# MLP output product by seven block products of eight, with sums of weight blocks made in DRAM by accumulating transfers

## What is computed

```python
h = rms_norm(x, pre_norm_mlp[l])
y = jnp.square(jax.nn.relu(h @ w_mlp_in[l])) @ w_mlp_out[l]   # (512, 4096) @ (4096, 1024)
x = x + rms_norm(y, post_norm_mlp[l])
```

## Time and profile before

| | |
|---|---|
| device time, median of three runs | 775.53 us (775.46 to 775.83) |
| span of the profiled execution, first to last instruction | 773.7 us |
| so outside the span, against the median | 1.8 us |
| PE busy | 765.9 us, 99% of the span |
| DVE, ACT, POOL busy | 329.9, 353.1, 387.1 us |
| data moved | 77.27 MB, mean 100 GB/s |

### The profile page before, as it was taken

The page is one execution under the profiler, slowest core; times in us unless marked ns, Lnnn a source line. Parts: engine busy times, 40 slices in busy tenths (PEclk is TensorE's granted clock), DMA queues, the critical chain, the costliest instruction groups (busy, mean ns, idle before and its releaser), DMA issues.

```text
span 773.7 us, 12234 instructions
## 1 busy us (share of the span) xinstructions
PE 765.9 (99%) x4276; PEld 628.5 (81%) x4276; DVE 329.9 (43%) x497; ACT 353.1 (46%) x625; POOL 387.1 (50%) x342
## 2 busy tenths in 40 slices
PE   9999999999999999999999999999999999999996
PEld 7788778888877878888888888888888888888885
DVE  5896899952544555546407210111013222222125
ACT  6656842286654464546336623333234333333333
POOL 2348884424437533664455545444544444444444
PEclk9999999999999999999999999999999999999999
DMA  9335233313222212223721333323332322222222
GB/s 332 97 97 190 63 88 96 98 53 97 56 55 63 74 43 56 83 96 117 265 81 55 95 109 96 93 83 108 95 96 95 105 98 95 95 95 95 95 81 110
DMA packets 59401, 77.27 MB, mean 100 GB/s; under 512 B 4544, under 2 KB 43616, under 8 KB 59360
## 3 DMA queue, kind: packets, MB, share of 16 engines
q1 hardware_dynamic: 59024, 76.44, 31.1%
q10 hardware_dynamic: 336, 0.28, 0.1%
HBM read 74.59 MB, written 2.11 MB: 99 GB/s over the span
## 4 chain that ended last, share of the span: by engine, by line
PE 91%; POOL 3%; DVE 2%; ACT 2%; issue 0%; DMA 0%; SPq 0%; ACTq 0%; POOLq 0%; DVEq 0%
PE bank L530 28%; PE bank L532 27%; PE bank L531 27%; POOL rsq L1598 2%; PE bank L755 1%; PE bank L778 1%; POOL w_lo L1604 1%; PE bank L765 1%; DVE y_out L1252 1%; PE bank L719 1%; DVE tmp L1516 1%; PE bank L683 1%; PE bank L560 1%; PE bank L730 1%; PE bank L827 0%
## 5 line engine op out<-in xcount | busy, mean ns | idle before, releaser
L1604 POOL TENSOR_TENSOR w_lo<-raw,w_hi 128x512 fp32r<-128x512 f32 x241 | 310.6, 1295 | 360.8 <-ACT w_hi L951 359.1
L951 ACT ACTIVATE w_hi<-raw 128x512 fp32r<-128x512 f32 (+1 forms) x246 | 153.3, 629 | 259.5 <-PE bank L532 254.4
L530 PE MATMUL bank<-h_hi,w_hi 128*128 128x512 f32 (+1 forms) x528 | 208.3, 395 | 0.1
L531 PE MATMUL bank<-h_lo,w_hi 128*128 128x512 f32 (+1 forms) x528 | 204.1, 387 | 0.0
L532 PE MATMUL bank<-h_hi,w_lo 128*128 128x512 f32 (+1 forms) x528 | 204.0, 386 | 0.0
L530 PEld LDWEIGHTS bank<-h_hi,w_hi 128*128 128x128 f32 x528 | 99.2, 188 | 24.8 <-issue 4.0
L532 PEld LDWEIGHTS bank<-h_hi,w_lo 128*128 128x128 f32 x528 | 99.2, 188 | 20.6
L531 PEld LDWEIGHTS bank<-h_lo,w_hi 128*128 128x128 f32 x528 | 99.3, 188 | 18.8
L530 PE MATMUL bank<-w_hi,a_hi 128*128 128x512 f32 x256 | 99.7, 389 | 0.1
L532 PE MATMUL bank<-w_hi,a_lo 128*128 128x512 f32 x256 | 99.6, 389 | 0.0
L531 PE MATMUL bank<-w_lo,a_hi 128*128 128x512 f32 x256 | 99.6, 389 | 0.0
(11 more groups left out here) (250 smaller groups left out, 888.0 us busy)
## 6 DMA issues: line engine op xcount, KB each, us to landing
raw<-in_w_in SPq DMA_DIRECT2D x87, 256.0 KB, 2.8
raw<-in_w_mlp_out SPq DMA_DIRECT2D x64, 256.0 KB, 2.5
raw<-in_w_mlp_in SPq DMA_DIRECT2D x62, 256.0 KB, 2.7
raw<-in_w_out SPq DMA_DIRECT2D x16, 256.0 KB, 2.7
x_sb<-in_x SPq DMA_DIRECT2D x4, 512.0 KB, 7.7
decay<-row_copy SPq DMA_DIRECT2D x4, 512.0 KB, 6.0
raw<-in_w_branch_att SPq DMA_DIRECT2D x8, 256.0 KB, 2.6
raw<-in_w_branch_dn SPq DMA_DIRECT2D x8, 256.0 KB, 2.7
```

Of the source, the lines that this page charges most:

```text
L530: pe.matmul(o, s_hi, m_hi, start=start, stop=False, skip_group_check=True)
L531: pe.matmul(o, s_hi, m_lo, start=False, stop=False, skip_group_check=True)
L951: return a.activation(o, i_, ACT.Copy, scale=scale)
L1604: g.tensor_tensor(w_lo[:, slot, :], raw[:, slot, :], w_hi[:, slot, :].bitcast(F32), ALU.subtract).then_inc(lo_ready, 1)
```

## The change

The output product is written as a 2 x 2 block product. A, the activations, is cut into token halves and into even and odd k-blocks of 128; B, the weights, into even and odd k-blocks and column halves (`w2_block(i, kappa, half)`). Seven block products are made instead of eight. The seven need sums of weight blocks and differences of activation blocks:

- v1 = B00 + B01, t3 = B11 + B01, t2 = v1 + B11, t4 = t2 + B10, each 2048 x 512 floats (4 MB) in DRAM, in eight pieces of 512 KB. Per piece and sum SP issues a DRAM to DRAM copy and POOL an accumulating transfer onto it: 32 of each. `SUM_AT` puts them at units 12 + 11 i + (0, 1, 8, 16) of the mixer, i = 0 to 7: the copy on SP behind the load of that unit, the add on POOL behind the subtraction for that unit. The copies of t2 and t4 wait for the add of v1 and of t2; every add waits for its copy. SP waits for all adds of v1, t3 and t2 before the first load of the output product, and for t4's before its second stage.
- Activations: `act` holds six blocks of 256 tokens per pair of k-blocks. ACT's squares write four of them, DVE makes three of 128x256 in `combine` during MLP in, and a fourth later (`s4`).
- The product has two stages in place of one. Stage one (`one`, eight turns): per turn two pairs of k-blocks by four weight parts, 8 parts of 6 matmuls. Stage two (`two`, seven turns and a tail): per turn 6 parts of 6 matmuls; the tail has 36 matmuls, ordered by output block. A **part** is a 128x512 weight tile; there are 64 + 48 = 112 of them where there were 64 units. Matmuls: 112 x 6 = 672 in place of 64 x 12 = 768.
- In both stages w_lo moves from POOL to DVE, two parts in one 128x1024 instruction; ACT's w_hi likewise. The parts have eight slots (`raw`, `raw_b`, `raw_c`), a_hi and a_lo are 128x1024 in stage one and 128x768 in stage two.
- Between the stages ACT copies two banks out and DVE makes six sums; after stage two the output blocks are put together by eight DVE additions, and squares, gain and residual follow per block.

The core of the diff:

```diff
 U_M1 = U_OUT + 64
-U_ALL = U_M1 + 64
+NI = 8
+S_TWO = 64
+N_SUM = 8
+SUM_AT = {12 + 11 * i + (0, 1, 8, 16)[q]: (q, i) for i in range(N_SUM) for q in range(4)}
...
-    act = at("act", 112, [P, FF // P, S])
+    act = at("act", 112, [P, 14, 6, 256])
+    act_end = at("act_end", 68, [P, 2, 6, 256])
...
+    v1_sum, t3_sum, t2_sum, t4_sum = [nc.dram_tensor(f"{name}_sum", (FF // 2, 512), F32).ap() for name in ("v1", "t3", "t2", "t4")]
+    w2 = w_mlp_out[0]
+    def w2_block(i, kappa, half):
+        c, n = slice(half * 512, half * 512 + 512), FF // N_SUM
+        return w2[i * n:i * n + n, c].rearrange("(j k p) c -> k p j c", k=2, p=P)[kappa]
+    def t_block(t, i):
+        n = FF // 2 // N_SUM
+        return t[i * n:i * n + n, :].rearrange("(j p) c -> p j c", p=P)
+    def t_copy(q, i):
+        t = (v1_sum, t3_sum, t2_sum, t4_sum)[q]
+        source = (w2_block(i, 0, 0), w2_block(i, 1, 1), t_block(v1_sum, i), t_block(t2_sum, i))[q]
+        return t_block(t, i), source
+    def t_add(q, i):
+        t = (v1_sum, t3_sum, t2_sum, t4_sum)[q]
+        return t_block(t, i), (w2_block(i, 0, 1), w2_block(i, 0, 1), w2_block(i, 1, 1), w2_block(i, 1, 0))[q]
...
             load(u, u % RAW, unit_source(u), u - RAW + 1 if u >= RAW else None)
+            if u in SUM_AT:
+                q, i = SUM_AT[u]
+                if q > 1:
+                    sp_.wait_ge(t_added[2 * q - 4], 16 * (i + 1))
+                sp_.dma_start(*t_copy(q, i)).then_inc(t_copied[q], 16)
...
+        def one_source(i, s):
+            n = i * 2 + s // 4
+            return (w2_rows(n, 0, 0), t_rows_of(t2_sum, n), t_rows_of(t3_sum, n), t_rows_of(v1_sum, n))[s % 4]
+        def two_source(i, s):
+            n = i * 2 + s // 3
+            return (w2_rows(n, 1, 0), w2_rows(n, 1, 1), t_rows_of(t4_sum, n))[s % 3]
...
-        def mlp_out_part(j, t, start, stop):
-            c = slice(t * P, t * P + P)
-            return three(bank[2 * t + j % 2][:], a_hi[:, j // 2, c], a_lo[:, j // 2, c], w_hi[:, j % 4, :],
-                         w_lo[:, j % 4, :], start, stop)
-        def mlp_out(i, first, last):
-            for j in range(4 if last else 8):
-                if j % 2 == 0:
-                    pe.wait_ge(alo_ready, i * 4 + (j // 2 + 1))
-                pe.wait_ge(lo_ready, i * 8 + (U_M1 + j - 1))
-                for t in (2, 3, 0, 1):
-                    if first and j == 0 and t < 2:
-                        pe.wait_ge(relu_done, 30 + 2 * t)
-                    x_ = mlp_out_part(j, t, first and j < 2, False)
-                x_.then_inc(unit_done, 1)
...
+        def product(bank0, p, c, i2, s, start, stop):
+            w0 = c * 256 + i2 * P
+            return three(bank[bank0 + i2][:], a_hi[p][:, w0:w0 + P], a_lo[p][:, w0:w0 + P], *w_part(s), start, stop)
+        def one(i, first=False, last=False):
+            for p in range(2):
+                pe.wait_ge(alo_ready, i * 2 + (p + 1))
+                for c in range(4):
+                    s = 4 * p + c
+                    pe.wait_ge(part_lo, i * 8 + (s + 1))
+                    if first and p == 0 and c > 1:
+                        pe.wait_ge(relu_done, 30 if c == 2 else 32)
+                    for i2 in range(2):
+                        x_ = product((4, 6, 0, 2)[c], p, c, i2, s, first and p == 0, last and p == 1)
+                    x_.then_inc(part_done, 1)
+        def two(i, first=False):
+            for p in range(2):
+                pe.wait_ge(alo_ready, i * 2 + (2 * NI + p + 1))
+                for c in range(3):
+                    s = 3 * p + c
+                    pe.wait_ge(part_lo, i * 6 + (S_TWO + s + 1))
+                    if first and p == 0:
+                        pe.wait_ge((p1_copied, x_made, y_made)[c], 2)
+                    for i2 in range(2):
+                        x_ = product((4, 6, 0)[c], p, (1, 0, 2)[c], i2, s, first and p == 0, False)
+                    x_.then_inc(part_done, 1)
+        one(0, True)
+        with pe.Fori(1, NI - 1) as i:
+            one(i)
+        one(NI - 1, False, True)
+        two(0, True)
+        with pe.Fori(1, NI - 1) as i:
+            two(i)
+        pe.wait_ge(alo_ready, 4 * NI)
+        for c, i2 in ((2, 0), (2, 1), (0, 0), (1, 0), (0, 1), (1, 1)):
+            for p in range(2):
+                s = {2: 0, 0: 2, 1: 6}[c] + p
+                if i2 == 0:
+                    pe.wait_ge(part_lo, S_TWO + 6 * (NI - 1) + {2: 2, 0: 4, 1: 0}[c] + p + 1)
+                x_ = product((4, 6, 0)[c], 2 * p, (1, 0, 2)[c], i2, s, False, p == 1)
+            x_.then_inc(tail_done, 1)
...
+        def two(i, before):
+            for g in range(3):
+                a.wait_ge(part_done, before + 2 * g + 2)
+                if g:
+                    a.wait_ge(s4_ready, i * 2 + g)
+                    a_split(i * 2 + (g - 1), g - 1, slice(3, 6))
+                w_split(2 * g, 2, i * 16 + (16 * (NI + 1)))
...
+        last_two = S_TWO + 6 * (NI - 2)
+        a.wait_ge(s4_ready, 2 * NI)
+        a_split(2 * NI - 1, 2, slice(3, 6))
+        w_split(6, 2, 16 * (NI + 1))
+        a.wait_ge(part_done, last_two + 2)
+        w_split(0, 2, 16 * (2 * NI))
+        a.wait_ge(part_done, last_two + 4)
+        a_split(2 * NI - 2, 0, slice(3, 6))
...
+        def combine(n):
+            x = [act_pair(n, slice(s, s + 1)).rearrange("p a c -> p (a c)") for s in range(6)]
+            v.tensor_tensor(x[3], x[2], x[5], ALU.subtract).then_inc(comb_one, 1)
+            v.tensor_tensor(x[2], x[0], x[2], ALU.subtract)
+            v.wait_ge(comb_one, n + 1)
+            v.tensor_tensor(x[1], x[0], x[3], ALU.subtract).then_inc(comb_ready, 1)
+        def s4(n):
+            x = [act_pair(n, slice(s, s + 1)).rearrange("p a c -> p (a c)") for s in (1, 4, 3)]
+            v.tensor_tensor(x[2], x[0], x[1], ALU.subtract).then_inc(s4_ready, 1)
+        def a_low(n, b, slots, ready):
+            c = slice(0, (slots.stop - slots.start) * 256)
+            v.wait_ge(ahi_ready, ready)
+            v.tensor_tensor(a_lo[b][:, c], act_row(n, slots), a_hi[b][:, c].bitcast(F32), ALU.subtract).then_inc(alo_ready, 1)
+        def w_low(s, n, ready):
+            v.wait_ge(part_hi, ready)
+            h, l = w_parts(s, n)
+            v.tensor_tensor(l, raw_part(s, n), h.bitcast(F32), ALU.subtract).then_inc(part_lo, n)
+        def one(i):
+            for g in range(4):
+                w_low(2 * g, 2, i * 8 + (2 * g + 2))
+                if g % 2:
+                    a_low(i * 2 + g // 2, g // 2, slice(0, 4), i * 2 + (g // 2 + 1))
+        def two(i):
+            for p in range(2):
+                s4(i * 2 + p)
+            for g in range(3):
+                if g:
+                    a_low(i * 2 + (g - 1), g - 1, slice(3, 6), i * 2 + (2 * NI + g))
+                w_low(2 * g, 2, i * 6 + (S_TWO + 2 * g + 2))
...
+        relu(NI - 1, ms=(0, 1))
+        combine(2 * NI - 4)
+        combine(2 * NI - 3)
+        a_low(0, 0, slice(0, 4), 1)
+        for s in range(3):
+            w_low(s, 1, s + 1)
+        relu(NI - 1, ms=(2, 3))
+        w_low(3, 1, 4)
+        w_low(4, 2, 6)
+        a_low(1, 1, slice(0, 4), 2)
+        w_low(6, 2, 8)
+        for n_ in (2 * NI - 2, 2 * NI - 1):
+            v.wait_ge(act_ready, 2 * n_ + 2)
+            combine(n_)
+        with v.Fori(1, NI - 1) as i:
+            one(i)
+        one(NI - 1)
...
+        def times_norm(t, half):
+            c = slice(half * 512, half * 512 + 512)
+            mark(v.tensor_tensor(y_out[:, t, c], half_of(t, half), pn_mlp[:, c], ALU.mult), y_scaled)
+        def finish(t, c, n_):
+            v.wait_ge(rsf_ready, n_)
+            mark(stt(y_out[:, t, c], y_out[:, t, c], rs1[:, t:t + 1], x_res[:, t, c], ALU.mult, ALU.add), y_final)
+        for i2 in range(2):
+            link(v.tensor_tensor(half_of(i2, 1), half_of(i2, 1), bank[2 + i2][:], ALU.add))
+            times_norm(2 + i2, 1)
+        for i2 in range(2):
+            v.wait_ge(tail_done, i2 + 1)
+            mark(v.tensor_tensor(half_of(2 + i2, 0), bank[i2][:], half_of(2 + i2, 0), ALU.subtract), y_half)
+            times_norm(2 + i2, 0)
+        for i2 in range(2):
+            v.wait_ge(tail_done, 2 * i2 + 3)
+            mark(v.tensor_tensor(half_of(i2, 0), bank[4 + i2][:], half_of(i2, 0), ALU.add), y_half)
+            if i2 == 0:
+                finish(2, slice(0, D), 1)
+            else:
+                times_norm(1, 0)
+            v.wait_ge(tail_done, 2 * i2 + 4)
+            mark(v.tensor_tensor(half_of(i2, 1), half_of(i2, 1), bank[6 + i2][:], ALU.subtract), y_half)
+            if i2 == 0:
+                finish(3, slice(0, D), 2)
+                times_norm(0, 0)
+                times_norm(0, 1)
+            else:
+                times_norm(1, 1)
+                finish(0, slice(0, D), 3)
+                for half in range(2):
+                    finish(1, slice(half * 512, half * 512 + 512), 4)
...
+            if u in SUM_AT:
+                q, i = SUM_AT[u]
+                g.wait_ge(t_copied[q], 16 * (i + 1))
```

(18 more changed lines are left out.)

242 lines of the change are left out of this document (168 added, 74 removed).

## The result

| | before | after |
|---|---|---|
| device time, median of six runs each | 775.5 us | 777.78 us (776.3 to 780.11) |
| span of the profiled execution | 773.7 us | 776.2 us |
| ratio after to before | | 1.003, 95% interval 1.0017 to 1.0043 |

The account below looks back on a forecast made before the run. PE was taken to bound the kernel, by the number of matmuls at 0.227 us each. 773.7 - 21.8 + 2.6 + 8.0 + 4.2 = 766.7, with 1.8 outside the span 768.5 us, 0.9% faster; range 761 to 775.

Parts of the forecast that it names:

- Term 1: Output product: 96 fewer matmuls of the same shape at 0.227 us each, -21.8 us.
- term 2: Output product, stages one and two: no other engine than PE binds them, 0 us.
- rival C: Output product: DVE binds it at 2.5 us per 1024-wide instruction, some 62 us more, 830 us; chance 0.03.
- Term 3: Hand-over from MLP in to the output product: PE waits for DVE's preparation, +2.6 us, ends 0 and 4.
- term 4: End of the kernel: DVE's last low parts, additions, multiplications and residual steps finish later, +8.0 us, ends 5 and 9.
- Term 5: Mixer's POOL-bound stretch: POOL's 32 accumulating transfers delay PE, +4.2 us, ends 0.5 and 10.5.
- X: POOL's time for one accumulating transfer: 1.3 us taken, ends 0.47 and 2.9.
- r: Mixer: lateness of the decay rows, broadcast loads behind the new copies, 1.5 us, ends 0 and 3.
- outside this stretch the other 28 fit in POOL's rest: Beyond the POOL-bound stretch, the other 28 adds hide in POOL's rest and its three-unit lead.
- Term 6: Copies and adds as DMA traffic, 34 MB in some 300 us on queues about a third busy: 0 us.
- rival D: Adds take over 19 us to land and SP stands behind them with the loads; at 20 us 784; chance 0.03.
- Rival B: Dear adds on POOL from 65 to 108 us: at 5.8 us each 782.0 us, slower than before; over 777: 0.08.

Follow-up runs that it names:

- the powers: On the changed kernel with its 32 copies but no adds, POOL raises five columns of ones to a power in place of each add: 772.69 us.
- small adds: The changed kernel with each of its 32 adds cut to 16 of the block's 512 columns: 774.82 us.

## Why the prediction was wrong

**Term 1 (-21.8) and term 2 (0) held.** MLP out is bound by PE at 0.227 us a matmul, with one gap of 1.4 us in 145 us; w_lo of 1024 on DVE took 1.23 us, a_lo of 768 took 0.96 (1.25 and 1.0 forecast), DVE was busy 106.90 of 145 us, and POOL 0. The division of rows 9 by rows 10 was right, and rival C is out.

**Term 3 (2.6) was 1.6; term 4 (8.0) was 9.3.** In term 4 I let PE's wait for the fourth a_lo be hidden by what follows. It came as 2.4 us, for ACT had first waited for `raw_c`. It brought a stretch at half clock, but that was hidden: as the sum of 169.5 us with either clock shows, DVE's chain ended last, as the term had it, and it is this chain that took 1.3 more than I had given it. Term 3 is inside its ends, term 4 just outside (5 to 9). Without the sums the rest of the forecast stood at 764.3, and 765.04 was measured.

**Term 5 (4.2) failed; it was 13.4 in the span.** X was right: 1.3 forecast, 1.2 measured. The formula was nearly so: X + (2X + r - 1.2) with X = 1.2 and the true r gives 7.9, and the matmul at 109 us was 7.45 late. (With the powers, where POOL began the decay blocks 4.2 us late, it gives 6.6, and 5.6 was measured; with small adds 8.0 and 7.1.) What failed is **r, the lateness of the decay rows: 1.5 with an upper end of 3, and it was 5.5.** I had looked for it in the transfers alone. They gave 3.1 with the copies only, just over my upper end; the rest came from an engine I did not ask, DVE, whose `sp` steps come before the rows and stood behind POOL at 41 to 46 us. The adds that held it there are among the 28 that I had put outside the stretch.

**And the sentence "outside this stretch the other 28 fit in POOL's rest" failed.** It asked what an add does to POOL and not what it does to DVE behind POOL: 2.0 us by way of the solve, at 147 us. It also took the clock as given: two stretches at 1.2 GHz in the mixer, over 1.5 us each, had no term. With 7.45, that is 12.5 of the 13.4.

**Term 6 (0) was about 4, and these 4 are part of the 13.4:** 0.9 for the copies, by way of r, and 3.0 for the bytes of the adds. The latter show at one place: the matmul of 147.46 waited 1.9 us, with small adds 0.5, for DVE came to its `qk_att` step 1.9 us later (146.72 against 144.80). It had met POOL more often on the way, whose add at 125.26 had waited 1.2 us for its copy. The low clock behind that wait, which the small adds did not have, is half of the 3.0. SP waited for `t_added` once, 0.3 us (an add landed in 8.3 us, not 19), so rival D is out. Rival B had the right place and the right sign, but its cause, dear adds, is refuted: the adds cost what I said, and the time was lost by whom they delayed.

My own signs were blunt. "PE waiting after 110 us for w_lo" was to be the mark of adds that do not hide, and there are 2.83 us at 116.72. But this is the matmul of 109.27, and a stall of some 4 us there was my sign of being right. What decides is that it was 7.45 late, and that PE waited at 147.46 for a step of DVE, which no sign named.
